# A half-row product of constants in the stream of the wide projections, once per 384 products

## What is computed

```python
def swiglu(hn, w_gu, w_down):                    # first block, D_FF = 2816
    g, u = jnp.split(hn @ w_gu, 2, axis=-1)
    return (jax.nn.silu(g) * u) @ w_down

def swiglu_2(h, w_in, w_out):                    # second block, D_FF_2 = 2816
    a, b = jnp.split(h @ w_in, 2, axis=-1)
    return (jax.nn.silu(a) * b) @ w_out

y = (g[:, :, 0] * (o_a @ w_up_a[l]) + g[:, :, 1] * (o_b @ w_up_b[l])
     + g[:, :, 2] * (o_c @ w_up_c[l]))
x = x + y @ w_out[l]
```

## Time and profile before

| | us |
|---|---|
| median of 3 executions | 3154.09 |
| lowest, highest | 3146.55, 3159.89 |
| the profiled execution | 3161.07 |
| its span, first to last instruction | 3158.7 |
| busy: PE, PEld, DVE, ACT, POOL | 2987.8, 2814.4, 1967.9, 1233.8, 261.9 |

### The profile page before, as it was taken

The page is one execution under the profiler, slowest core; times in us unless marked ns, Lnnn a source line. Parts: engine busy times, 40 slices in busy tenths (PEclk is TensorE's granted clock), DMA queues, the critical chain, the costliest instruction groups (busy, mean ns, idle before and its releaser), DMA issues.

```text
span 3158.7 us, 55499 instructions
## 1 busy us (share of the span) xinstructions
PE 2987.8 (95%) x23214; PEld 2814.4 (89%) x23214; DVE 1967.9 (62%) x3125; ACT 1233.8 (39%) x2095; POOL 261.9 (8%) x318
## 2 busy tenths in 40 slices
PE   8898989999898989999998989999999998999899
PEld 7788889978797989999876689999999998887899
DVE  5755688465567857767576556665565655445655
ACT  4454554445455444222335233223322233235443
POOL 1311000122101000000111210000100001000000
PEclk9999999999999999999999999999999998999899
DMA  6434467533355754554231115544244443242454
GB/s 199 123 107 147 134 208 242 169 115 109 109 170 178 241 183 154 186 175 160 90 108 52 41 54 167 177 154 144 95 160 161 138 143 101 94 147 87 131 186 130
DMA packets 245597, 447.66 MB, mean 142 GB/s; under 512 B 14483, under 2 KB 87076, under 8 KB 244580
## 3 DMA queue, kind: packets, MB, share of 16 engines
q1 hardware_dynamic: 239584, 430.79, 42.1%
q10 hardware_dynamic: 5764, 13.33, 1.3%
HBM read 443.01 MB, written 1.05 MB: 141 GB/s over the span
## 4 chain that ended last, share of the span: by engine, by line
PE 80%; DVE 10%; ACT 5%; issue 3%; POOL 1%; DMA 1%; ACTq 0%; DVEq 0%; SPq 0%; POOLq 0%
PE ps L1121 64%; DVE split L1818 3%; PE ps L1149 2%; PE ps L1150 2%; PE ps L1151 2%; ACT split L1525 2%; DVE A L1815 1%; DVE AR L1818 1%; ACT A L1615 1%; PE ps L1055 1%; DVE small L1988 1%; PE ps L1274 1%; PE ps L1363 1%; DVE A L1856 1%; PE ps L1249 1%
## 5 line engine op out<-in xcount | busy, mean ns | idle before, releaser
L1121 PE MATMUL ps<-AR,split 128*128 128x256 f32 x19392 | 2340.5, 282 | 29.6 <-DVE A L1815 8.7
L1121 PEld LDWEIGHTS ps<-AR,split 128*128 128x128 f32 x19392 | 2282.0, 190 | 78.9 <-issue 38.3
L1818 DVE TENSOR_TENSOR split<-raw,split 128x1024 fp32r<-128x1024 f32 (+1 forms) x710 | 786.4, 1150 | 603.3 <-ACT split L1525 595.4
L1525 ACT ACTIVATE split<-raw 128x1024 fp32r<-128x1024 f32 (+2 forms) x728 | 681.6, 986 | 793.7 <-PE ps L1121 672.4
L2060 DVE SCALAR_TENSOR_TENSOR junk<-A,cb 128x1024 bf16<-128x1024 f32 x144 | 175.7, 1220 | 42.3 <-DMA A<-w_modT 40.1
L2060 DVE SCALAR_TENSOR_TENSOR A<-A,cb 128x1024 f32<-128x1024 f32 x144 | 175.4, 1218 | 0.0
L2296 POOL TENSOR_TENSOR A<-A 128x256 f32<-128x256 f32 (+1 forms) x45 | 39.8, 884 | 1584.4 <-ACT A L1535 1571.9
L1818 DVE TENSOR_TENSOR AR<-A,AR 128x256 fp32r<-128x256 f32 (+2 forms) x252 | 147.0, 584 | 23.6 <-ACT AR L1589 7.8
L1577 ACT ACTIVATE AR<-A 128x256 fp32r<-128x256 f32 (+1 forms) x132 | 68.4, 526 | 194.5 <-DVE A L1910 194.5
L1815 DVE SCALAR_TENSOR_TENSOR A<-A,ps 128x256 f32<-128x256 f32 (+1 forms) x196 | 95.2, 505 | 61.4 <-ACT A L1573 56.3
L1573 ACT ACTIVATE A<-ps 128x256 f32<-128x256 f32 (+1 forms) x132 | 63.3, 490 | 140.1 <-PE ps L1121 139.8
(11 more groups left out here) (231 smaller groups left out, 2298.6 us busy)
## 6 DMA issues: line engine op xcount, KB each, us to landing
A<-w_modT SPq DMA_DIRECT2D x144, 512.0 KB, 4.3
raw<-w_in SPq DMA_DIRECT2D x120, 512.0 KB, 4.5
raw<-w_gu SPq DMA_DIRECT2D x80, 512.0 KB, 4.6
raw<-ffn_a_in SPq DMA_DIRECT2D x80, 512.0 KB, 4.3
raw<-ffn_b_in SPq DMA_DIRECT2D x80, 512.0 KB, 4.3
raw<-ret_in SPq DMA_DIRECT2D x48, 512.0 KB, 4.3
raw<-w_down SPq DMA_DIRECT2D x44, 512.0 KB, 5.1
raw<-ffn_a_out SPq DMA_DIRECT2D x44, 512.0 KB, 4.4
```

Source lines behind the costliest of these rows:

```text
L1121: mm = e.matmul(out[:, s:s + NT], wt[:, c, m_], xs(k0 + c, a + s, a + s + NT), start=first and part + s == 0, stop=last and part == 2 and ...
L1525: e.activation(hi, self.raw_view(q), ACT.Copy).then_inc(*self.mark(("w hi", q)))
L1818: return self.e.tensor_tensor(out, v, hi.bitcast(F32), ALU.subtract)
```

## The change

`TensorE` gets a counter, `streak`. Ahead of each block of a wide projection `pause` is called with the number of products in the block. Where the counter has reached 384 it is set to 0 and one product is issued: `ones` on 64 rows by 512 elements of `base` on 64 rows, plain float32, into bank 7, behind a wait for what was last in that bank, if anything was. Nothing reads the result. After a block that is led by a norm the counter is set to 383.

```diff
     def start(self):
         e = self.e
+        self.streak = 0
         e.wait_ge(*self.after("ones"))
...
+    def pause(self, i, products):
+
+        if self.streak >= 384:
+            self.streak = 0
+            if self.K.held.get(7) is not None:
+                self.e.wait_ge(*self.after(("free", self.K.held[7])))
+            self.e.matmul(self.banks[7][:, 0:512], self.ones[0:64, :], self.base[0:64, 0:512], start=True, stop=True)
+        self.streak += products
...
                     self.catch_up()
                     yield
+                self.streak = 383
                 continue
+            if group is WIDE:
+                self.pause(i, 3 * nk * (n // P) * (T // NT))
             for m in range(n // P):
```

## The result

The kernel after takes **3187.03 us** (3175.63 to 3187.26, five runs) where the kernel before took 3154.09 on the same chip (3146.55 to 3159.89): a ratio of 1.0098, with an interval of 1.0067 to 1.0129. Forecast were 3200 us in a range of 3183 to 3226, and slower with 0.93. The sign and the range held; the loss was 33 us and not 46.

A forecast was written before the change was run, and what follows sets the result against it. TensorE, busy 95% of 3158.7 us mainly with projection products, was taken as the bound. The profiled 3161.1 us plus 53.3 for 42 added products less 14.4 for shorter steps gave 3200 us, range 3183 to 3226.

The forecast's parts named there:

- What bounds the kernel, and that nothing hides the product: TensorE, busy 95% of 3158.7 us, never waits in dense wide-projection streams, so all 53.3 us of added products count.
- The number, 42: Walking the counter through the wide projection calls gives 42 added products among 14,880 wide ones.
- Sum 0.20 + 0.54 + 0.52 + 0.12, less 0.11: 1.27 us: Price per added product, from the filter's last products: entry, between halves, exit, settling, less one ordinary step; 53.3 us for 42.
- The lower bound, 0.86 us: Least price of one added product, read from a full-row f32 product of 512 in the wide stream; 36 us for 42.
- the rival without a drain: Entering and leaving half rows does not drain TensorE: price 0.86 us each, same rhythm gain, 3183 us; chance 0.10.
- I take 12% of the products as long behind: Wide products left at the long step after the change: 8 us remain of 22.4, so a gain of 14.4 us.
- The base: Time the forecast's changes were added to: the profiled execution of the kernel before, 3161.1 us.
- I suspect that executions differ in just that: The 13.3 us spread of the kernel before comes from wide streams' short or long step; one 3072-product stream makes 13.8.
- The kernel after should spread less: With the added products setting the step, execution times should vary less than the 13.3 us of the kernel before.
- Rhythm untouched: Rival: each added product costs 1.27 us but wide streams resume at their former step, 3214 us; chance 0.13.
- Mostly long: Rival: wide streams mostly take long steps behind the added product, 3259 us if all, 3226 if half; chance 0.12.
- Runs beside: Rival: the half-row product overlaps neighbouring wide products on TensorE, so no change, 3157 us; chance 0.05.

The follow-up runs named there:

- Twice as often: Kernel after with its 64-row, 512-element product once per 192 wide products instead of 384, 77 products instead of 42: 3228.05 us, ratio 1.0236.
- full-row run: Kernel after with the added product on all 128 rows instead of 64, at the same 42 places: 3215.03 us, ratio 1.0181.

## Why the prediction came out right, and where it was off

**What bounds the kernel, and that nothing hides the product: right.** Twice as often shows it: 35 more cost 41 us of the 44.3 that their price makes. The sign rested on this alone, since 53.3 us of price stand against at most 22.4 of gain. A few products may hide, in the four short wide stages of before that wait anyway (one product each, changes of -1.2 to 0.0 us). "Nothing hides it" was too strong by up to the 5 us that these four cost elsewhere.

**The number, 42: right**, with 84 halves.

**"Sum 0.20 + 0.54 + 0.52 + 0.12, less 0.11: 1.27 us": right**, 1.267 measured. The filter's last products were the right row to read, since they have shape, rows and type in common. The lower bound, 0.86 us from the full-row product of the earlier trace rows, was 0.852 to 0.879 when it was run in this place. So the half rows themselves cost 1.267 - 0.86 = 0.41 us, and the rival without a drain falls. By the Trainium skill, "TensorEngine Tiling (Array Packing)" (Key Properties), a change of the tiling mode drains the engine; the runs agree: 0.206 us in against 0.115 for full rows, the second half 0.533 behind the first against 0.428, and 0.741 (0.519 and 0.222) from the second half to the second wide product against 0.545 (0.027 and 0.518). The page has no price. The in and out that remain with 16 elements, 0.540 in all, are that price for a product that does nearly nothing. The weight loads show what is lost on the way in. In the full-row run the product's own loads begin while the wide products still run, 0.12 us ahead of it (start, us, line, count):

```profile
1048.87 0.31 PEld L1053 LDWEIGHTS ps<-base,ones 128*128 128x128 f32 x2
1048.98 1.02 PE L1053 MATMUL ps<-base,ones 128*128 128x512 f32 x2
```

In the kernel after, the first load and the first half start together, at 306.2 in the source view above and 2 ns apart in the trace: the half-row product's load isn't taken ahead.

**"I take 12% of the products as long behind": the term that was mis-sized, and the picture behind it was wrong.** The prediction counted 23 places entered short with 17 left short, and 32 entered long with 14 left short, and made a draw of it. Those places have products of several lengths and numbers between the streams. For one kind of product nothing is drawn: from a short stream 512 elements on half the rows leave a short one every time, and from a long one the phase decides. With a map that never leaves the short rhythm and leads out of the long one after one or two products, a stream ends short after a few products and stays there. In the kernel after the six stages of the table above hold 564 such steps among 13,546 products, 4% and not 12%. All long steps went from 7,480 to 2,750, a gain of 21.0 us and not 14.4; the 8% are 5 us of these 6.6. But 20.6 us of the gain lay in the two streams that were short ahead of their first product. That they were is luck, and the size of the gain in this pair of profiles doesn't confirm the mechanism; the table of phases does. The seven of eight places with 512 elements pointed there, and were weighted too little.

**The base.** The prediction added its change to the profiled execution, 7 us over the median, and that execution was a draw with some long streams. The balance: +53.2 as forecast, -21.0 instead of -14.4, -5.5 where products hide or the low clock differs, gives +26.7 on the profiled spans; the medians, 3154.09 and 3187.03, are 33 apart.

**"I suspect that executions differ in just that": right in part.** Three profiles of the kernel before have three different sets of long streams, with 7,480 to 10,268 long steps, 12.4 us apart. But 23 executions of it on one chip go from 3131.61 to 3172.68 us, 41 us, so the rhythm isn't all, and that it matched the first spread of 13.3 us was chance. **"The kernel after should spread less": not shown.** Its five runs spread by 11.6 us and its four by 21.6, with 2,750 and 2,928 long steps in the profiles of the two. Its rhythm hardly differs between these two profiles, so most of what spreads in it seems to be something else, which wasn't found.

**Rivals.** *Rhythm untouched* (3214) falls by the long streams that turned short right at a half-row product (7 of 12 with 512 elements, 7 of 11 with 128), where no dense stream of over 1,000 products changed by itself in the three profiles of the kernel before. In the kernel after alone it would have been nearly right: 37 of 37 short streams go on as they were. *Mostly long* (3226 to 3259) is what full rows do, not half rows: 13,577 long steps. *Runs beside* falls with the price. *No drain* gave 3183, 4 us from the result, for the wrong reason: a price too low and a gain too small cancel.

**Open.** What sets a stream's rhythm at its entry, behind the waits of the norm-led block, wasn't found: it differs between executions of one program. Nor was why the phase is mapped as it is, and why the length of the product changes the map. A change of the entry itself wasn't tried. Nor was a version that catches all three phases at six or twelve products.

## What to carry to other kernels

A product put between others costs what it moves its neighbours' starts apart, and not its columns: 1.27 us for two halves that follow each other in 0.43 us when they have all rows, with 0.54 us left at 16 elements. Before a periodic fix is added, compare the most that it could give (here 384 x 0.0045 = 1.7 us per product, and that only in the streams that are long, about a third of the products) with that price; a correction that lasts for thousands of products needs to be made once, and even once it gained nothing that 12 runs could show. And when one program's executions differ, read two profiles of it before the one is taken as the state that a change acts on.

## What the runs showed that was not expected

The dense stream of one kind of product has **two stable steps, 113.33 and 117.78 ns**, at the same clock of 1.00 and with the same instructions, and keeps either for 3,000 products. The long one has a period of three, with one weight load of 192 ns among two of 188. In the Trainium skill, "TensorE: Matmul & The Clock Gate" (Back-to-back issue gap) gives N / 2.4 + 2.5 ns, an estimated 109.2 ns for 256 columns, and calls it the gap of isolated products. For streams of weight loads and products it names about 81 ns at 128 columns and 131 at 512, and none at 256. The runs show neither stream at 109.2, and both are longer.

A full-row product of plain float32 turns every short stream into a long one (34 of 34), a half-row product of the same length none (0 of 205 with either of two lengths). The weight loads around one full-row product that left its stream long (1048.5 to 1049.0 us of the full-row run), in the view of one tile's loads (ns, least, median, most):

```profile
L1134 PEld LDWEIGHTS ps<-AR,split x4: 188/188/192, 1048.4 to 1048.8; 128*128 128x128 f32 x4
L1053 PEld LDWEIGHTS ps<-base,ones x2: 188/190/192, 1048.9 to 1049.0; 128*128 128x128 f32 x2
```

In the first line one of the last four loads of the stream took 192 ns, and in the second one of the product's own two did. In the profile this duration is the only sign of the phase; the step of a stretch (350 or 364 products in 41 us) tells the rhythm, and the loads tell where in it a product falls.
